# Key projection first, clears on ScalarE, feature blocks turned by TensorE and a contiguous routing stage in a hybrid S5 / RWKV-7 / MoE layer

## The chip, the core and the metric

The kernel runs on one core of a Trainium2 chip. The metric is the time of one execution in device microseconds, 1267.28 us before the change (median of 3 runs, 1266.63 to 1267.98). Below, PE is TensorE's matmul queue, PEld its weight loads, DVE is VectorE, ACT ScalarE, POOL GpSimd and SP SyncE, whose queue issues nearly all transfers.

## The reference

One decoder layer over 256 tokens of 1024 features, in f32:

```python
h = rms_norm(x, norm_mix_g)
proj = h @ w_in                       # columns: S5 input u, then r, k, v (512 each)
y_s5 = s5_mixer(proj[..., :r0], ...)  # 32 groups of 16 channels, 64 complex states each
y_rw = rwkv7_mixer(h, r, k, v, ...)   # 8 heads of 64: decay, iclr and gate LoRAs, delta rule
x = x + concat(y_s5, y_rw) @ w_out
x = x + moe_ffn(rms_norm(x, norm_moe_g), ...)   # top 4 of 32 experts, clamped SwiGLU
x = x + (p @ ple_w_proj) * sigmoid(rms_norm(x, norm_ple_g) @ ple_w_gate)
return rms_norm(x, final_norm_g)
```

The mixture computes every expert's three 1024x1024 f32 products for the tokens routed to it, so all 32 experts' weights are read (12 MB each).

## The kernel before, in words

The program is written by hand: each engine has its own list of instructions in the order of the code, and semaphores tie them. `layer` is the part up to the router's first logits; `experts` holds the routing stage, the loop over the experts and the tail, as three blocks, each of which begins when all engines have left the one before. All data lie in one on-chip array, `arena`, of 47 units of 1024 floats per partition; `un(i, n)` is n units from i, and names share units one after the other.

Head: SP loads the parameters, x transposed, the constants, then the eight quarters of `w_in` in the table `order` with the LoRA weights behind the second. POOL clears the padded S5 operands (L307 to L309) and, after the second projection, the taps (L317). ACT squares x (L325), computes step sizes and phases; DVE works out the S5 coefficients in many 16-element instructions (from L496) and inverts the root (L550). PE sums the squares with the ones of the constants.

Projections: `project(n)` makes quarter `order[n]`, `copy_proj(n)` on ACT moves it out of its bank. Before, the order is u, u, k, k, r, r, v, v. Between them PE does the LoRA products (all through banks 5 and 6), `kernel_taps` (the S5 output kernel, behind `o_padded`), `turn_g` (transposes the padded kernels, with an ACT copy of each), `stack_u` and `into` (S5 states' input). DVE runs `products` (S5 operands), `token_shift` (r, k, v with their predecessors), the decay's running sum, the normalised keys, `phase_off` and `phase_on` (rotation and scan of the S5 states, in two halves).

Scores: for 16 units (4 chunks of 64 tokens, 4 pairs of heads) PE computes five 64x64 products with `pair` (one product per head of the pair), DVE masks them. Then come five levels that invert a triangular matrix: per level and half PE makes W = MO X and Y W, ACT copies W, DVE adds to X and transposes it. Behind the levels 1 to 3, `turn` on DVE transposes bh, kh and v into `Bs`, `Ks`, `Vs` (L700, eight instructions each), and `s5_out` / `s5_y` make the S5 output. Then follow the scan over the four chunks, the normalisation of its output, `w_out` and the residual add (L795).

Routing (`experts`, first block): x normalised is split into three bf16 parts, written in the order that the weights' rows have ("run order"), so that the gather by one-hot matmuls is exact; `by_run` and `plain` are the two views. Tile 0 is split on DVE (`part`, L1210 to L1215), tile 1 by ACT (L1182 to L1190) and POOL (L1261, L1263). The logits are used at L1222 on DVE, then come the top 4, the mask (L1236), the ranks by a triangular matmul, and the number of passes (L1254). PE also makes three of the four products of the per-layer embedding (`ple_proj`), which ACT copies (L1193), and opens the output banks with products of zeros. SP loads the last two of the six weight chunks of expert 0.

Expert loop: each chunk of the ring is asked for again as soon as its matmuls are done:

```python
sp.wait_ge(s["chunks_used"], (n - 1) * NC + c + 1)
sp.dma_start(slot(c), chunk_src(c, e)).then_inc(chunk_in[c], 16)
```

## Time and profile before

| | |
|---|---|
| median of 3 runs | 1267.28 us |
| the profiled execution | 1267.05 us |
| its span | 1265.3 us |
| PE / PEld / DVE / ACT / POOL busy | 1170.8 / 514.8 / 402.3 / 205.1 / 28.3 us |
| routing block, from PE's first transpose | 260.76 us |
| PE's first loop matmul | 295.69 us |
| first load issued by the loop | 299.58 us |

Times in the rows are microseconds from the span's start. A row of the timeline gives start, duration, engine, line, operation, output and inputs with shapes, how often (x), and in brackets the idle time of the engine before it and who ended it. Durations of POOL are rough, and busy PE is not PE at its peak.

### The profile page before, as it was taken

The numbers are of one execution on the slowest core, as the hardware profiler recorded it, in microseconds if no ns is written. First come the engines' busy times: TensorE is split into PE (matmuls) and PEld (weight loads), VectorE is DVE, ScalarE is ACT, GpSimd is POOL, SyncE is SP. The second block draws the span as 40 slices with busy tenths as digits, with TensorE's granted clock in tenths as the row PEclk, the third lists the DMA queues.
The fourth block names the chain that finished last, engine by engine and source line by source line (L and its number), as shares of the span: only waits on it lengthen the run. The fifth ranks groups of instructions, "written<-read, shape, count | busy, mean of one in ns | idle before, by whom it ended". The sixth has DMA issues, their size and how long they took to land. (4 is left out here: it accounts for less than half of the span.)

```text
span 1265.3 us, 19269 instructions
## 1 busy us (share of the span) xinstructions
PE 1170.8 (93%) x8190; PEld 514.8 (41%) x8190; DVE 402.3 (32%) x750; ACT 205.1 (16%) x297; POOL 28.3 (2%) x16
## 2 busy tenths in 40 slices
PE   5889688958999999999999999999999999999997
PEld 4678586433333333333333333333333333333333
DVE  8928992572112122122112112211212112211222
ACT  2661012262000010011000001000011000000113
POOL 4100000020000000000000000000000000000000
PEclk8899888979999999999999999999999999999998
DMA  9300207235999999999999999999999999999960
GB/s 326 99 2 3 71 19 292 100 146 223 419 427 426 429 429 428 428 429 428 427 429 430 427 428 430 428 428 429 429 427 429 429 428 427 430 428 427 429 273 33
DMA packets 44237, 429.38 MB, mean 339 GB/s; under 512 B 4817, under 2 KB 15441, under 8 KB 19633
## 3 DMA queue, kind: packets, MB, share of 16 engines
q1 hardware_dynamic: 44016, 428.43, 80.9%
q8 instruction: 23, 0.38, 0.1%
q0 software_dynamic: 192, 0.52, 0.1%
q14 instruction: 6, 0.04, 0.0%
HBM read 427.89 MB, written 1.05 MB: 339 GB/s over the span
## 5 line engine op out<-in xcount | busy, mean ns | idle before, releaser
L1140 PE MATMUL bank<-arena 128*64 128x512 f32 (+5 forms) x5388 | 920.6, 479 | 24.7 <-DMA arena<-in_exp_w_up 19.1
L1140 PEld LDWEIGHTS bank<-arena 128*64 128x64 f32 (+4 forms) x5388 | 316.3, 128 | 605.3 <-issue 541.9
L221 PE MATMUL bank<-arena 64*64 64x64 f32 (+7 forms) x2032 | 175.0, 282 | 27.2 <-DVE arena L603 7.8
L221 PEld LDWEIGHTS bank<-arena 64*64 64x64 f32 (+3 forms) x2032 | 141.6, 160 | 59.8 <-issue 40.8
L1331 ACT ACTIVATE arena<-arena 128x512 f32<-128x512 f32 x32 | 20.1, 629 | 515.4 <-DVE arena L1375 515.4
L1390 DVE COPY arena<-bank 128x512 f32<-128x512 f32 x32 | 22.1, 691 | 234.9 <-PE bank L1140 234.9
L1380 DVE TENSOR_SCALAR arena<-bank 128x512 f32<-128x512 f32 x32 | 22.1, 691 | 211.8 <-PE bank L1140 211.8
L1375 DVE TENSOR_SCALAR arena<-bank 128x512 f32<-128x512 f32 x32 | 22.1, 691 | 188.8 <-PE bank L1140 188.8
L1334 ACT ACTIVATE arena<-bank 128x256 f32<-128x256 f32 x32 | 12.3, 383 | 310.1 <-PE bank L1430 310.1
L1351 DVE TENSOR_TENSOR arena<-bank,par 128x512 f32<-128x512 f32 x33 | 22.8, 692 | 76.4 <-PE bank L1140 76.4
L1331 ACT ACT_TABLE_LOAD x32 | 41.1, 1283 | 1.7 <-PEq L1162 1.2
L1383 DVE SCALAR_TENSOR_TENSOR arena<-arena 128x512 f32<-128x512 f32 x32 | 33.7, 1054 | 1.1
L1378 DVE TENSOR_TENSOR arena<-arena 128x512 f32<-128x512 f32 x32 | 22.1, 692 | 24.5 <-ACT arena L1331 24.5
L221 PE MATMUL bank<-arena,con 128*32 128x64 f32 (+2 forms) x160 | 17.5, 302 | 12.6 <-DMA con<-in_consts 10.4
L1336 ACT ACTIVATE arena<-bank 128x512 f32<-128x512 f32 x32 | 19.1, 597 | 1.7
L1363 DVE TENSOR_SCALAR arena<-con,arena 128x128 f32<-128x128 f32 x64 | 19.3, 344 | 0.0
L1434 PE MATMUL bank<-con,arena 128*128 128x128 f32 x128 | 19.2, 273 | 0.0
L1348 DVE TENSOR_SCALAR arena<-con,arena 128x64 bf16<-128x64 f32 x66 | 13.8, 251 | 13.3 <-DVE arena L1369 7.0
L700 DVE STREAM_TRANSPOSE arena<-arena 32x512 f32<-32x512 f32 x24 | 16.7, 697 | 0.3
L1430 PEld LDWEIGHTS bank<-con,arena 128*128 128x128 f32 x64 | 6.4, 141 | 24.3 <-issue 24.3
L221 PEld LDWEIGHTS bank<-arena,con 128*32 128x32 f32 (+1 forms) x160 | 9.5, 138 | 16.6 <-DMA con<-in_consts 10.4
L439 ACT ACTIVATE arena<-bank 128x512 f32<-128x512 f32 x10 | 6.0, 597 | 57.5 <-PE bank L221 57.5
(269 smaller groups left out, 459.8 us busy)
## 6 DMA issues: line engine op xcount, KB each, us to landing
arena<-in_exp_w_gate SPq DMA_DIRECT2D x64, 2048.0 KB, 23.4
arena<-in_exp_w_down SPq DMA_DIRECT2D x64, 2048.0 KB, 21.8
arena<-in_exp_w_up SPq DMA_DIRECT2D x64, 2048.0 KB, 25.3
arena<-in_w_in SPq DMA_DIRECT2D x8, 1024.0 KB, 12.1
arena<-in_w_out SPq DMA_DIRECT2D x4, 1024.0 KB, 5.5
arena<-in_ple_w_gate SPq DMA_DIRECT2D x2, 2048.0 KB, 21.7
arena<-in_xT SPq DMA_DIRECT2D x1, 1024.0 KB, 6.1
arena<-in_lora SPq DMA_DIRECT2D x1, 1024.0 KB, 13.6
```

Of the source, the lines that this page charges most:

```text
L221: return nc.tensor.matmul(out, lhsT, rhs, start=start, stop=stop, skip_group_check=True)
L1140: return nc.tensor.matmul(out, lhsT, rhs, start=start, stop=stop, skip_group_check=True)
L1331: nc.scalar.activation(sg, gt, ACT.Sigmoid, scale=1.702).then_inc(s["sig_ready"], 1)
L1336: nc.scalar.activation(actT[:, :, :, :], GATE[:, :].rearrange("p (k h s) -> p k h s", h=2, k=4), ACT.Copy).then_inc(s["actT_ready"], 1)
L1351: tt(xg[:, :, :], GAT[:, :].rearrange("p (k s) -> p k s", k=KD), prm("g_moe_run")[:, :, None].to_broadcast([P, KD, SLOTS]), ALU.mult).then ...
L1363: ts(pg[:, t, :], iota, rank[:, t, bass.ds(e, 1)], gates[:, t, bass.ds(e, 1)], ALU.is_equal, ALU.mult).then_inc(s["pg_ready"], 1)
L1375: ts(gt, GATE[:, :], 7.0, None, ALU.min).then_inc(s["gt_ready"], 1)
L1378: tt(sg, sg, gt, ALU.mult).then_inc(s["swish_ready"], 1)
L1380: ts(up, UP[:, :], 7.0, -7.0, ALU.min, ALU.max).then_inc(s["up_read"], 1)
L1383: stt(by_run(gt), plain(up), 1.0, plain(sg), ALU.add, ALU.mult).then_inc(s["act_ready"], 1)
L1390: V.tensor_copy(y, YB[:, :]).then_inc(s["y_ready"], 1)
L1434: last = nc.tensor.transpose(GATE[:, k * P:(k + 1) * P], gt[:, k * P:(k + 1) * P], ident)
```

## The change

It touches `layer` and the first block of `experts`, in nine pieces.

1. The order of the quarters becomes k, k, u, u, r, r, v, v. All waits that name a place in it go by `at_place`.
2. All clears leave POOL. ACT writes zeros (`clear`): a copy of the epsilon column times 0. Two are ahead of the step sizes, one between the exponentials, two behind the squares, the taps' one behind the output padding. The squares now stand behind the phases.
3. PE sums squares with ones that DVE writes (`ones_early`), not those of the constants.
4. The LoRA's second products use banks 5/6, 2/3, 5/6; the third stands behind `project(2)`. The key norms' sums stand behind `project(3)`; taps, turns, stack and both `into` stand behind `project(5)`.
5. ACT and DVE follow: on ACT the square of the keys, the decay's exponentials and the key norms' root come ahead of the output padding and the phases' sines; on DVE keys, decay and k2 come ahead of the output `products` (whose units change to 37, 25, 39), and `phase_off(0)`, `phase_on(0)` come behind r.
6. `turn` moves to PE (behind Y W of the levels 0, 1, 2), with ACT copying out of banks 0 and 1.
7. ACT adds the root of each tile's mean square to the square (`x2_root`); DVE splits tile 0 between its residual adds: one float write in run order, then contiguous casts and subtracts.
8. In the routing block DVE does the same for tile 1 (two casts on ACT), POOL does nothing there.
9. `ple_proj(0)` comes ahead of the logits, `ple_proj(1)` and `(2)` ahead of the ranks, each in a bank of its own; the products of zeros come last.

```diff
-        order = [0, 1, 4, 5, 2, 3, 6, 7]
+        LORA_BANK = (5, 2, 5)
+        order = [4, 5, 0, 1, 2, 3, 6, 7]
+        at_place = [order.index(q) + 1 for q in range(8)]
...
-                nc.gpsimd.memset(un(45), 0.0).then_inc(s["pads_clear"], 1)
-                nc.gpsimd.memset(un(16, 4), 0.0).then_inc(s["pads_clear"], 1)
-                nc.gpsimd.memset(un(20, 4), 0.0).then_inc(s["pads_clear"], 1)
...
+                def clear(a, n):
+                    A(un(a, n), par[:, NPARAM:NPARAM + 1].to_broadcast([P, n * UNIT]), ACT.Copy, scale=0.0).then_inc(s["pads_clear"], 1)
+                act.wait_ge(s["eps_ready"], 1)
+                clear(45, 1)
+                clear(16, 2)
...
+                clear(18, 2)
...
+                act.wait_ge(s["xT_in"], 16)
+                for b in range(2):
+                    A(sq[:, 4 * b:4 * b + 4, :], xT[:, 4 * b:4 * b + 4, :], ACT.Square).then_inc(s["sq_ready"], 1)
+                clear(20, 2)
+                clear(22, 2)
...
+                    if lev < 3:
+                        for b in range(2):
+                            act.wait_ge(s["turn_done"], 2 * lev + b + 1)
+                            A((Bs, Ks, Vs)[lev][:, 8 * b:8 * b + 8, :], banks[b].rearrange("p (u t) -> p u t", t=CH), ACT.Copy).then_inc(s["turned"], 1)
...
-                    A(un(33 + t), x2[:, t, :], ACT.Square, accum_out=ssq[:, t:t + 1])
+                    link(A(xn[t], x2[:, t, :], ACT.Square, accum_out=ssq[:, t:t + 1]))
+                    A(inv[:, t:t + 1], ssq[:, t:t + 1], ACT.Sqrt, bias=par[:, NPARAM:NPARAM + 1], scale=1.0 / D).then_inc(s["x2_root"], 1)
...
+                residual(0)
+                residual(1)
+                dve.wait_ge(s["x2_root"], 1)
+                link(V.reciprocal(inv[:, 0:1], inv[:, 0:1]))
+                link(ts(by_run(xn[0]), plain(x2[:, 0, :]), inv[:, 0:1], None, ALU.mult))
+                residual(2)
+                link(V.tensor_copy(parts[:, 0, 0, :], xn[0]))
+                link(tt(xres[0], xn[0], parts[:, 0, 0, :], ALU.subtract))
+                link(V.tensor_copy(parts[:, 0, 1, :], xres[0]))
+                tt(xres[0], xres[0], parts[:, 0, 1, :], ALU.subtract)
+                residual(3)
...
+                lora_second(0)
+                lora_second(1)
                 project(2)
+                lora_second(2)
+                project(3)
+                head_sums(kksq, 4).then_inc(s["kk_summed"], 1)
+                project(4)
+                project(5)
                 kernel_taps()
                 turn_g()
                 stack_u()
-                project(3)
                 into(0)
                 into(1)
...
+                def turn(n):
+                    if n == 0:
+                        pe.wait_ge(s["bonus_ready"], 1)
+                    pe.wait_ge(s["scaled"], 4)
+                    for b in range(2):
+                        if n:
+                            pe.wait_ge(s["turned"], 2 * n - 2 + b + 1)
+                        for u in range(8 * b, 8 * b + 8):
+                            last = pair(banks[b][:, (u % 8) * CH:(u % 8 + 1) * CH], fm((bh, kh, vv)[n], u), con[:, C_ID2:C_ID2 + CH])
+                        last.then_inc(s["turn_done"], 1)
...
+            nc.scalar.activation(parts[:, 0, 2, :], xres[0], ACT.Copy)
             act.wait_ge(s["rest_ready"], 1)
-            nc.scalar.activation(by_run(parts[:, 1, 1, :]), plain(xres[:, 1, :]), ACT.Copy).then_inc(s["parted"], 1)
+            nc.scalar.activation(parts[:, 1, 1, :], xres[1], ACT.Copy).then_inc(s["parted"], 1)
```

PE's list around the second LoRA products and the projections that follow. `win_in_*` are the quarters' loads. Before:

```order
L221 MATMUL bank<-lora_hidden,arena 128x256 [waits lora_hidden_ready]
L221 MATMUL bank<-lora_hidden,arena 128x256 x3
L221 MATMUL bank<-lora_hidden,arena 128x256 [waits lora2_copied,lora_hidden_ready]
L221 MATMUL bank<-lora_hidden,arena 128x256
L221 MATMUL bank<-lora_hidden,arena 128x256 [waits lora2_copied]
```

and with the change:

```order
L231 MATMUL bank<-lora_hidden,arena 128x256 [waits lora_hidden_ready]
L231 MATMUL bank<-lora_hidden,arena 128x256 x3
L231 MATMUL bank<-lora_hidden,arena 128x256 [waits lora_hidden_ready]
L231 MATMUL bank<-lora_hidden,arena 128x256 x3
L231 MATMUL bank<-arena 128x256 [waits proj_copied,win_in_u0]
L231 MATMUL bank<-arena 128x256 x15
L231 MATMUL bank<-lora_hidden,arena 128x256 [waits lora2_copied,lora_hidden_ready]
L231 MATMUL bank<-lora_hidden,arena 128x256
```

The second kind no longer waits for `lora2_copied`, and u's first quarter stands ahead of the third.

DVE's list in level 1 (L688 and L709 the masks, L745 and L756 the additions to X, L624 and L637 `s5_y`). Before:

```order
L688 TENSOR_TENSOR arena<-arena,con 128x512 [waits w_done] x2
L745 TENSOR_TENSOR arena<-arena,bank 128x512 [waits xy_done]
L692 STREAM_TRANSPOSE arena<-arena 128x512 [waits xy_ready]
L745 TENSOR_TENSOR arena<-arena,bank 128x512 [waits xy_done]
L692 STREAM_TRANSPOSE arena<-arena 128x512 [waits xy_ready]
L700 STREAM_TRANSPOSE arena<-arena 32x4x4x32 x8
L624 SCALAR_TENSOR_TENSOR arena<-arena,par,bank 128x4x64 [waits s5_out_done]
```

and with the change:

```order
L709 TENSOR_TENSOR arena<-arena,con 128x512 [waits w_done] x2
L756 TENSOR_TENSOR arena<-arena,bank 128x512 [waits xy_done]
L713 STREAM_TRANSPOSE arena<-arena 128x512 [waits xy_ready]
L756 TENSOR_TENSOR arena<-arena,bank 128x512 [waits xy_done]
L713 STREAM_TRANSPOSE arena<-arena 128x512 [waits xy_ready]
L637 SCALAR_TENSOR_TENSOR arena<-arena,par,bank 128x4x64 [waits s5_out_done]
```

The eight transposes of L700 are gone; PE's list has 32 products of 64x64 with `con` as moving operand in their place.

DVE's list from the last residual adds to the logits. Before:

```order
L795 TENSOR_TENSOR arena<-arena,bank 128x512 [waits out_done,x_in]
L795 TENSOR_TENSOR arena<-arena,bank 128x512 [waits out_done] x3
...
L1210 TENSOR_SCALAR arena<-arena 128x1024
L1211 CAST arena<-arena 128x2x128x4 [waits m_dve]
L1212 TENSOR_TENSOR arena<-arena 128x1024 [waits m_dve]
L1213 CAST arena<-arena 128x2x128x4 [waits m_dve]
L1214 TENSOR_TENSOR arena<-arena 128x1024 [waits m_dve]
L1215 CAST arena<-arena 128x2x128x4 [waits m_dve]
L1222 SCALAR_TENSOR_TENSOR arena<-bank,arena 128x32 [waits m_logits_done,m_router_in,m_dve]
```

and with the change, in the routing block:

```order
L1235 RECIPROCAL small<-small 128x1
L1236 TENSOR_SCALAR arena<-arena,small 128x2x128x4 [waits m_dve]
L1237 CAST arena<-arena 128x1024 [waits m_dve]
L1238 TENSOR_TENSOR arena<-arena 128x1024 [waits m_dve]
L1243 SCALAR_TENSOR_TENSOR arena<-bank,small,arena 128x32 [waits m_logits_done,m_router_in]
```

Three casts in run order became one float write in run order and one contiguous cast; the rest stands ahead of the fourth residual add or behind the mask.

## Rows read from the trace of the kernel before

**Rows 1.** Windows by stage: stretch, length; busy us (x) of PE, PEld, DVE, ACT, POOL; clock; DMA share; GB/s
```profile
260.00:290.00 30.00, 14.71 (x52) 8.81 (x52) 24.07 (x35) 20.39 (x21) 7.68 (x2) 0.66 0.41 154
...
321.00:600.00 279.00, 279.00 (x1690) 99.31 (x1688) 57.57 (x130) 28.92 (x40) 0.00 (x0) 1.00 1.00 427
```

**Rows 2.** Timeline of the head: start, duration, engine, line, operation, out<-in [idle before]
```profile
2.74 8.70 DVE L496 TENSOR_SCALAR s5p<-par 128x16 f32<-128x16 f32 x1 [1.82 <-DMA par<-in_params]
...
7.88 3.53 POOL L309 MEMSET arena<- 128x4096 f32 x1
...
10.36 6.55 PE L221 MATMUL bank<-arena,con 128*128 128x256 f32 x16 [10.36 <-DMA con<-in_consts]
...
18.84 1.75 DVE L550 RECIPROCAL arena<-arena 128x256 f32<-128x256 f32 x1
```

**Rows 3.** Timeline of the projections and the first scores
```profile
55.72 3.75 PE L221 MATMUL bank<-lora_hidden,arena 128*128 128x256 f32 x8 [3.88 <-ACT arena L372]
...
89.48 1.22 DVE L630 TENSOR_TENSOR arena<-arena 128x1020 f32<-128x1020 f32 x1 [22.82 <-ACT arena L358]
...
105.93 0.69 DVE L663 TENSOR_SCALAR arena<-arena 128x1024 f32<-128x1024 f32 x1 [5.15 <-ACT arena L432]
...
119.18 2.33 DVE L613 TENSOR_TENSOR_SCAN arena<-arena 128x512 f32<-128x512 f32 x2
...
125.34 0.60 ACT L358 ACTIVATE arena<-bank 128x512 f32<-128x512 f32 x1 [6.31 <-PE bank L221]
...
134.91 0.68 DVE L713 TENSOR_TENSOR arena<-bank,con 128x512 f32<-128x512 f32 x1
...
135.14 9.41 PE L221 MATMUL bank<-arena 64*64 64x64 f32 x256 [7.82 <-DVE arena L603]
```

**Rows 4.** Timeline of the levels, and the start of the chunk scan
```profile
158.93 11.75 PE L221 MATMUL bank<-arena 64*64 64x64 f32 x328 [2.00 <-DVE arena L745]
...
166.24 5.68 DVE L700 STREAM_TRANSPOSE arena<-arena 32x512 f32<-32x512 f32 x8
...
176.31 5.67 DVE L700 STREAM_TRANSPOSE arena<-arena 32x512 f32<-32x512 f32 x8
...
195.89 1.97 PE L221 MATMUL bank<-arena 64*64 64x64 f32 x32 [5.29 <-ACT arena L441]
```

**Rows 5.** Windows of PE: stretch, length, busy us (x records), granted clock, DMA share, GB/s
```profile
56.00:58.00 2.00, 2.00 (x6) 0.50 0.00 0
...
161.00:162.00 1.00, 1.00 (x24) 0.50 0.00 0
...
169.00:170.00 1.00, 1.00 (x41) 1.00 0.00 0
```

**Rows 6.** Timeline of the routing stage and the loop's start
```profile
258.60 0.69 DVE L795 TENSOR_TENSOR arena<-arena,bank 128x512 f32<-128x512 f32 x1 [3.62 <-PE bank L221]
...
268.32 2.74 DVE L1213 CAST arena<-arena 128x1024 bf16<-128x1024 f32 x1
...
278.15 0.41 DVE L1222 SCALAR_TENSOR_TENSOR arena<-bank,arena 128x32 f32<-128x32 f32 x2
...
278.92 2.40 DVE L1227 TENSOR_SCALAR arena<-arena 128x2 f32<-128x2 f32 x1
...
286.19 0.15 DVE L1254 TENSOR_SCALAR arena<-arena 128x1 int32<-128x1 f32 x1
...
278.44 2.85 POOL L1263 TENSOR_TENSOR arena<-arena 128x1024 f32<-128x1024 f32 x1 [4.89 <-ACT arena L1184]
...
285.15 5.67 PE L1140 MATMUL bank<-arena,lora_hidden 128*128 128x512 f32 x8
...
290.86 0.60 ACT L1193 ACTIVATE arena<-bank 128x512 f32<-128x512 f32 x1 [1.32 <-PE bank L1140]
...
295.69 18.03 PE L1140 MATMUL bank<-arena 128*64 128x512 f32 x80 [0.87 <-DVE arena L1351]
```

**Rows 7.** The page's costliest groups: one run-order write in the loop
```profile
L1383 DVE SCALAR_TENSOR_TENSOR arena<-arena 128x512 f32<-128x512 f32 x32 | 33.7, 1054 | 1.1
```

More of the change, by code:

```diff
@@ L679, in _ @@
                 V.memset(state[:, :], 0.0)
+                phase_off(0)
+                phase_on(0)
                 phase_off(1)
@@ L908, in _, with head_sums @@
                             last.then_inc(s["lora2_done"], 1)
-                project(2)
+                def head_sums(src, bank):
+                    for b in range(2):
+                        last = mm(banks[bank + b][:, :], head_ones, src[:, 2 * b:2 * b + 2, :], True, True)
+                    return last
+                lora_second(0)
+                lora_second(1)
+                project(2)
+                lora_second(2)
+                project(3)
+                pe.wait_ge(s["consts_in"], 16)
+                pe.wait_ge(s["kk_squared"], 1)
+                pe.wait_ge(s["lora2_copied"], 6)
+                head_sums(kksq, 4).then_inc(s["kk_summed"], 1)
+                project(4)
+                project(5)
                 kernel_taps()
@@ L1277, in _ @@
             last.then_inc(s["logits_done"], 1)
-            pe.wait_ge(p_in, 32)
-            ple_proj(0, banks[5]).then_inc(s["ple_done"], 1)
+            for n in range(1, EARLY):
+                ple_proj(n, banks[n]).then_inc(s["ple_done"], 1)
             pe.wait_ge(s["mask_ready"], 1)
```

233 lines of the change are left out of this document (98 added, 135 removed).

## The prediction

> **What bounds the kernel now.** I read the page's 40 slices first: from slice 11 on, DMA stands at 9 and TensorE at 9, before that neither does. The table of stages says it in numbers [rows 1]: in the expert loop PE is busy 279.00 of 279.00 us at a granted clock of 1.00, and the DMA engines' share is 1.00. The change leaves every line of that loop and of the tail as it is, and the loop's loads are released by its own matmuls, so the loop moves as a block: **what counts is when it begins**, 295.69 us before [rows 6]. Then I read the timeline of each engine from 0 to 296 us and asked at each hand-over which engine came last. There are four places.
>
> First, the head. VectorE's second useful instruction, 16 elements wide, takes 8.70 us, and ends where POOL's last clear ends (7.88 + 3.53 = 11.41) [rows 2]. VectorE's chain of small instructions follows, and the first reciprocal starts at 18.84, though ScalarE's root was there earlier.
> Second, the projections. VectorE idles 22.82 us for the keys' copy, until 89.48; PE idles 3.88 us before 55.72, behind ScalarE, and then runs at a clock of 0.50 [rows 3, 5]. PE ends the projections at 125.3, and after the first scores waits 7.82 us until 135.14 for VectorE, whose score masks start at 134.91 [rows 3].
> Third, the inversion's levels. PE waits at each for VectorE, 2.00 us at the second, and VectorE has eight 32-row transposes there, 5.68 us a time, three times [rows 4]. After each wait PE runs at 0.50 (1.2 of 2.4 GHz): 24 records a microsecond against 41 at 1.00 [rows 5].
> Fourth, routing. The logits' first use on VectorE is at 278.15, behind casts of 2.74 us into run order; then ScalarE's last copy at 290.86 waits for PE's late small projections (8 records, 5.67 us) [rows 6]. The mean clock there is 0.66 [rows 1].
>
> **The head.** ScalarE now clears 1024 + 2048 + 2048 elements before its squares and 4096 behind them. At 0.60 us for 512 (the last copy [rows 6]) that is about 1 us per 1024. It clears from 2.0 to 5.0, then one exponential, 2.0 more of clearing, two exponentials, a table load of 1.3 and two sines: the squares run 9.5 to 11.5 instead of from 7.4. PE no longer waits for the constants; it starts at the first half, 10.6 instead of 10.36, takes the same 6.55 [rows 2], and the root is out at 17.7. VectorE, without the 8.70 us, is done by 14.5. So the reciprocal starts at 17.7 instead of 18.84: **-1.1 us**. This queue is a new wait: ScalarE's clears are in front of the squares. Bounds 0 (if the 8.70 us stays) and -2.
>
> **The projections.** PE's queue keeps the work and loses the holes: the second LoRA products of the first two kinds go to banks of their own, the third stands behind a projection. Gone are 3.88 us of idling, some 2.9 us lost at 0.50 behind it [rows 5], and 1.1 us of small gaps. What stays is the hole while ScalarE empties the transposed kernels. With the head, PE ends the projections 9.0 us earlier: 116.3.
> Is anything else later? I laid the changed lists of all engines against each other, with the durations that the same instructions have in the timeline. ScalarE: exponentials of the decay to 65, the root of the key norms at 69.3, padding of the S5 outputs to 73.6, clear to 75.5, sines and copies to 83.1; PE reaches the taps at 81.3, so o_padded is 7 us early and the last copy (83.1) is in time for its reader, VectorE's r. VectorE: g products to 46.7, then keys 51, decay 56.3, k2 59.5, output products 67, phase angles 72.8, then the chain that took 105.93 to 119.18 [rows 3], 13.25 us: 86.0. r and its products to 91.9. Then it waits: PE's first into() ends at 99.3. phase_off(0), phase_on(0), phase_off(1) take 3.8 + 6.4 + 3.7: 113.2, before PE's 116.3. So PE sets the masks' start, 1.0 us of first scores later: 117.4 instead of 134.91, **-17.5 us** with the head. PE feeds the masks at the pace of before, and the levels start at 131.6. Bound above: if VectorE is late after all, only PE's wait of 7.82 us comes back; below: -19.
>
> **The levels.** VectorE loses 3 x 5.68 us. PE gains 3 x 64 records (32 products of 64x64, two records each), at 41 a microsecond 1.56 us each, and ScalarE six copies of 0.6 us. Per level at full clock: 64 + 64 records, 64 more for the turn, and s5_out at 2.45 us, together 7.1 us instead of the 10.1 at which VectorE repeats (eight transposes at 166.24, the next at 176.31 [rows 4]). VectorE's own part is 4.7 (two masks, two additions, two transposes, s5_y), so PE has no hole once it is in step. From 131.6: level 0 at half clock to 136.3, turn and s5_out to 140.3, a wait of 1.2 us for X, which phase_on(1) holds back as before; level 1 to 149.3, level 2 to 156.4, level 3 to 162.0, level 4 to 165.1, VectorE to 166.5, Gelu to 167.6. The chunk scan starts at 168.0; I add 0.9 us, half of what another fall of the clock in level 1 costs, 168.9 instead of 195.89 [rows 4]: **another -9.5 us**. Bounds: all levels at half clock, 2.7 us a turn and 11.5 us a level, give nothing; no fall at all -10.5. I take the upper end of speed, since PE runs on through each level.
> The Trainium skill weighs against this (VectorE: DVE Perf Modes, "The three transpose paths" and "Rules for kernel authors"): a bf16 block of 128x128 takes 390 ns on TensorE and 311 ns on VectorE, and 32x32 blocks within a bank are fastest on VectorE. By that ratio 5.68 us would become 7.1 us of PE per turn. The rows of PE's small products (41 a microsecond) say 1.56, and the sum goes by them. The mechanism is a rival below.
>
> Chunk scan, normalisation and output projection are unchanged, so -27.0 holds to there. The weights they need are asked for earlier, and DMA is nearly idle.
>
> **Routing.** Times here on the clock of before. The last residual add was at 258.60 [rows 6]. Now VectorE has, between the second and the fourth: waiting for ScalarE's square and root of tile 0 until 253.1, a reciprocal, one run-order write, the third add, two contiguous casts and two subtracts. The write's nearest row is the loop's own run-order write, 1054 ns for 512 elements [rows 7], so 2.05 us for 1024; ends 0.69 (a plain one-input instruction of that size, first row of the 13.25 us chain [rows 3]) and 2.74 (the cast [rows 6]). A contiguous cast: 0.7 by that plain row, at most 2.74. Subtracts 1.23. The fourth add starts at 260.1: **+1.5**, and ScalarE's root behind its square adds 0.4: the block starts 1.9 later, 262.65. The third add is 1.1 late and nobody waits for it.
> In the block VectorE clears 0.9, writes 2.05, casts 0.7, subtracts 1.23: free at 267.7. PE: transposes, the first small projection now ahead of the logits, partly at 0.50 after its hole of 2.4 us (3.5 us full at that clock, 1.7 at 1.00), logits done at about 268.6. So the logits are used at 268.7 instead of 278.15. From there the mask took 4.8 us, of which 2.2 were one 2-element instruction of 2.40 us beside POOL's subtract, which is gone [rows 6]: 271.2. One more subtract 1.23, then 1.9, the ranks, 0.9: count at 275.2. PE in the meantime: two projections at 1.00 to 272.0, ranks to 273.6, the four clears of banks to 274.6 (they wait for ScalarE's third copy, 272.7). ScalarE's casts are 1.1 each instead of 4.8. The block ends at 275.2 instead of 291.46, and the hand-over to the loop, 4.2 us (290.86 + 0.60 to 295.69), stays: **-16.3 us**. Bounds: run-order writes at 2.74 and all at 0.50: -11; writes at 0.69: -19.
> A second rule of the skill (the same page, "Mode 2x_2P"): a one-input instruction between SBUF tensors runs two elements a cycle whatever the stride if the outer dimension is even. By it both writes would take 0.69 and the sum would be 2.7 us lower, 1221. The old casts with the same pattern took 2.74 [rows 6], so the trace does not agree.
>
> **Sum.** -17.5 - 9.5 - 16.3 = -43.3 us. The profiled execution took 1267.05 (span 1265.3 and 1.75 around it), 0.2 under the median of the three runs, 1267.28. 1267.1 - 43.3 = 1223.8, rounded to **1224**.
>
> **The rivals.**
> *VectorE still comes last before the scores* (phase_off(0) and everything behind it is now queued behind r, and into(0) behind two more projections). For: a margin of only 3 us in a chain of 70. Against: the rows' durations add up. It gives back up to the 7.82 us wait and a clock fall: 1233. Chance 0.10.
> *Casts stay slow* although contiguous, because it was the bf16 write and not the stride. Against: I find no contiguous f32 to bf16 cast in this trace, but float writes in run order are slow too [rows 7]. Two casts of 2.7 in front of the fourth add, one in the block, three of 4.8 on ScalarE in line with VectorE's: +10 us, 1234. Chance 0.09.
> *Turns are as dear on PE as on VectorE*: if 16 blocks of small products, their bank switches and the wait for ScalarE's copy take 5.68 us on PE too, a level is 5.6 + 5.68 = 11.2 us instead of 7.1, +12.3 over three: 1236. Against: 41 records a microsecond [rows 5]. Chance 0.03. By the ratio in the skill's table it would be 7.1 us a turn and 1241.
> *The change does not reach the end*: the loop's end would have to be fixed by its loads and not by its start. But the first load of the loop waits for the first chunk's matmuls, so it moves too; within 0.2%, chance 0.01.
> *Slower*: the loop itself loses the full clock. It runs PE without a gap [rows 1], so each microsecond at 0.50 costs nearly half a microsecond; 43 us are gone if the clock is at 0.50 for 87 us or more of the loop, and slower begins beyond about 92. At 120 us of it the kernel takes 1284. For it: PE now is busier in the 160 us ahead of the loop. Against: 1.00 throughout 321 to 600 us, and every fall of the clock in this trace follows a hole in PE's work. Chance 0.02.
>
> **How the numbers follow.** The forecast has 0.75, with its own ends 1217 (writes at 0.69, no clock fall) and 1230 (slow writes, half of the levels' gain). The range reaches to the first two rivals: 1217 to 1236. Faster by over 0.2% (2.5 us, about what can be told from no change): 0.97; within: 0.01; slower: 0.02.
>
> **What would show it.** VectorE's second instruction under 0.3 us and the reciprocal near 17.7; no hole of PE between 50 and 81; masks of the scores near 117.4, with PE, not VectorE, the last; a granted clock of 1.00 from level 1 on and 64 turn records in about 1.6 us; chunk scan near 169; logits used about 6 us after the block's start, against 17.4 before; contiguous casts near 0.7; PE's loop from 252.4 on. Wrong it would be if a wait on `into_done` or `phase_off` stands ahead of the scores, if casts keep 2.7 us, or if PE's wait of 2 us per level stays.

## The result, and the profile after

The changed kernel takes **1222.65 us** (median of 4 runs, 1220.94 to 1226.11), the kernel before, run beside it, 1267.63 (4 runs, 1266.63 to 1268.09): ratio 0.965, 95% interval 0.9625 to 0.9675. Forecast were 1224.0, range 1217 to 1236. The profiled execution took 1220.94 us (span 1219.2), 46.1 under the profiled one before, against -43.3 in the sum. So the total came out 2.9 us below the sum for that execution; its parts were off by more, in both directions.

The head, timeline of the changed kernel (start, duration, engine, line, operation, out<-in, count, [idle before <- who ended it]):

```profile
2.69 0.17 DVE L518 TENSOR_SCALAR s5p<-par 128x16 f32<-128x16 f32 x1 [1.66 <-DMA par<-in_params]
...
16.49 1.75 DVE L572 RECIPROCAL arena<-arena 128x256 f32<-128x256 f32 x1 [2.31 <-ACT arena L350]
...
2.04 2.85 ACT L330 ACTIVATE arena<-par 128x1024 f32<-128x1024 f32 x2
...
8.98 1.99 ACT L346 ACTIVATE arena<-arena 128x1024 f32<-128x1024 f32 x2
...
10.16 5.71 PE L231 MATMUL bank<-arena 128*128 128x256 f32 x16 [10.16 <-ACT arena L346]
```

The 8.70 us instruction of [rows 2] is down to 0.17. The reciprocal starts at 16.49 instead of 18.84, and now waits for ScalarE's root, as forecast (17.7). ScalarE's queue of clears is the new wait; it came 0.5 us earlier than the 9.5 I gave it.

Projections and first scores, timeline after:

```profile
97.90 0.69 DVE L611 TENSOR_TENSOR arena<-bank,arena 128x512 f32<-128x512 f32 x1 [2.27 <-PE bank L231]
...
108.53 0.69 DVE L611 TENSOR_TENSOR arena<-bank,arena 128x512 f32<-128x512 f32 x1 [0.27 <-PE bank L231]
...
115.34 0.60 ACT L372 ACTIVATE arena<-bank 128x512 f32<-128x512 f32 x1 [6.31 <-PE bank L231]
...
116.43 0.69 DVE L724 TENSOR_TENSOR arena<-bank,con 128x512 f32<-128x512 f32 x1 [4.08 <-PE bank L231]
```

The last copy of a projection is at 115.34 instead of 125.34, the first score mask at 116.43 instead of 134.91 [rows 3]. The bracket decides the first rival: VectorE waits 4.08 us for PE there, so VectorE is not last.

The levels, PE's timeline after:

```profile
130.24 5.50 PE L231 MATMUL bank<-arena 64*64 64x64 f32 x128 [3.54 <-DVE arena L709]
135.54 2.06 PE L231 MATMUL bank<-con,arena 64*64 64x64 f32 x64
...
141.42 3.02 PE L231 MATMUL bank<-arena 64*64 64x64 f32 x96 [0.17 <-DVE arena L756]
144.27 2.03 PE L231 MATMUL bank<-con,arena 64*64 64x64 f32 x64
...
152.38 2.03 PE L231 MATMUL bank<-con,arena 64*64 64x64 f32 x64
...
169.55 1.15 PE L231 MATMUL bank<-arena 64*64 64x64 f32 x32 [2.66 <-ACT arena L461]
```

The rows of inputs `con,arena` are the turns. The second and the third lie 8.11 us apart: that is the period of a level now, against 10.07 between the transposes of [rows 4]. The chunk scan starts at 169.55 instead of 195.89.

Windows of the two kernels. First before (busy us (x) of PE, PEld, DVE, ACT, POOL; granted clock; DMA share; GB/s):

```profile
20.00:48.00 28.00, 26.74 (x114) 21.13 (x115) 27.76 (x34) 5.72 (x7) 10.28 (x3) 0.89 0.80 257
...
195.00:200.00 5.00, 4.11 (x51) 3.84 (x52) 0.00 (x0) 0.93 (x2) 0.00 (x0) 0.50 1.02 433
...
235.00:240.00 5.00, 5.00 (x10) 2.18 (x9) 4.86 (x8) 0.69 (x1) 0.00 (x0) 0.70 1.07 453
```

and after, the same places of the program where they now lie, and the loop's entry:

```profile
20.00:48.00 28.00, 25.88 (x125) 20.46 (x123) 27.50 (x33) 6.27 (x11) 8.18 (x2) 1.00 0.80 258
...
168.00:173.00 5.00, 3.45 (x56) 2.94 (x56) 0.21 (x1) 1.44 (x2) 0.00 (x0) 1.00 1.02 412
...
205.00:210.00 5.00, 4.15 (x10) 2.00 (x11) 4.74 (x6) 1.48 (x3) 0.00 (x0) 1.00 1.04 437
...
246.00:250.00 4.00, 3.13 (x26) 1.25 (x24) 1.87 (x8) 0.00 (x0) 0.00 (x0) 0.55 0.34 114
250.00:254.00 4.00, 4.00 (x14) 1.26 (x12) 0.00 (x0) 0.00 (x0) 0.00 (x0) 0.60 0.00 0
```

The clock's column tells of two things that were not in the forecast. PE runs at 1.00 through the chunk scan and the start of the output projection, where it had 0.50 and 0.70. And it is at 0.55 to 0.60 at the loop's entry, behind a wait of 3.29 us, which costs there.

Routing and loop start, timeline after:

```profile
223.17 1.28 DVE L809 TENSOR_SCALAR arena<-arena,small 128x1024 f32<-128x1024 f32 x1
...
225.09 0.69 DVE L811 CAST arena<-arena 128x1024 bf16<-128x1024 f32 x1
...
236.42 0.41 DVE L1243 SCALAR_TENSOR_TENSOR arena<-bank,small,arena 128x32 f32<-128x32 f32 x2 [0.68 <-PE bank L1172]
...
237.19 0.17 DVE L1248 TENSOR_SCALAR arena<-arena 128x2 f32<-128x2 f32 x1
...
242.68 0.15 DVE L1277 TENSOR_SCALAR arena<-arena 128x1 int32<-128x1 f32 x1
...
245.01 1.62 PE L1172 MATMUL bank<-arena 128*128 128x64 bf16 x48 [3.29 <-DVE arena L1363]
...
247.49 20.85 PE L1172 MATMUL bank<-arena 128*64 128x512 f32 x80 [0.87 <-DVE arena L1366]
```

A contiguous cast takes 0.69 us against 2.74 [rows 6], the float write in run order 1.28, the 2-element instruction 0.17 against 2.40. The loop's products start at 247.49 instead of 295.69, but their first group takes 20.85 us instead of 18.03 [rows 6].

### The profile page after: what moved, and what is told of

Read it like the earlier page. It is cut to its first block and busy times, and to the rows that moved or that the text cites. A ratio compares the mean times of both kernels' runs of the same rounds, so it can differ in the third digit from the quotient of the medians.

```text
span 1219.2 us, 19644 instructions
## 1 busy us (share of the span) xinstructions
PE 1157.3 (95%) x8382; PEld 506.1 (42%) x8382; DVE 368.9 (30%) x730; ACT 207.3 (17%) x310; POOL 10.7 (1%) x10
## 5 line engine op out<-in xcount | busy, mean ns | idle before, releaser
L231 PE MATMUL bank<-arena 64*64 64x64 f32 (+7 forms) x2048 | 169.1, 267 | 22.6 <-ACT arena L346 10.2
L231 PEld LDWEIGHTS bank<-arena 64*64 64x64 f32 (+3 forms) x2048 | 135.5, 147 | 53.9 <-issue 40.1
L1351 ACT ACTIVATE arena<-bank 128x512 f32<-128x512 f32 x32 | 19.1, 598 | 1.7
L1449 PE MATMUL bank<-con,arena 128*128 128x128 f32 x128 | 19.2, 273 | 0.0
L1445 PEld LDWEIGHTS bank<-con,arena 128*128 128x128 f32 x64 | 6.4, 141 | 24.3 <-issue 24.3
L1449 PEld LDWEIGHTS bank<-con,arena 128*128 128x128 f32 x128 | 15.0, 140 | 0.0
L582 DVE SCALAR_TENSOR_TENSOR arena<-arena,par 128x256 f32<-128x256 f32 x16 | 14.1, 952 | 0.0
L1445 PE MATMUL bank<-con,arena 128*128 128x128 f32 x64 | 14.0, 301 | 0.0
L231 PE MATMUL bank<-arena,con 128*32 128x64 f32 (+1 forms) x144 | 10.3, 264 | 2.2 <-ACT arena L484 1.4
```

The costliest lines, as they stand in the source:

```text
L231: return nc.tensor.matmul(out, lhsT, rhs, start=start, stop=stop, skip_group_check=True)
L1445: last = nc.tensor.transpose(YB[:, t * P:(t + 1) * P], pg[:, t, :], ident)
L1449: last = nc.tensor.transpose(GATE[:, k * P:(k + 1) * P], gt[:, k * P:(k + 1) * P], ident)
```

## The experiments

The marks of all profiled executions, in us from each span's start. "Masks" is VectorE's first score mask, "scan" PE's first product of the chunk scan, "turn x2" PE's first transpose of the residual stream, "loop" the start of the loop's first group of float products, "group" how long that group of 80 records took. The ratios are to the runs of the kernel before that were taken beside each kernel (medians 1266.1 to 1267.6), and of each edit only the telling lines are printed. One profile is one execution: in `x2`, `x8` and `x12`, whose code up to the scores' products is that of the changed kernel, the masks start 0.7 to 0.9 us later than in it, with PE at 0.94 over 20 to 48 us (`x2`, `x12`) or 0.83 over 84 to 94 (`x8`), so a mark that moves by less than 1 us says nothing.

| kernel | masks | scan | turn x2 | loop | group | median (runs) | ratio to before, 95% |
|---|---|---|---|---|---|---|---|
| before | 134.91 | 195.89 | 254.09 | 295.69 | 18.03 | 1267.63 (4) | |
| after | 116.43 | 169.55 | 223.97 | 247.49 | 20.85 | 1222.65 (4) | 0.965 [0.9625, 0.9675] |
| xb, before + projections | 118.91 | 179.41 | 237.55 | 279.17 | 18.03 | 1249.94 (4) | 0.9861 [0.9845, 0.9878] |
| x5, before + turns on PE | 134.36 | 187.85 | 242.28 | 285.60 | 18.03 | 1256.63 (4) | 0.9918 [0.9901, 0.9934] |
| x4, before + routing | 134.78 | 195.80 | 254.01 | 279.59 | 18.03 | 1250.48 (4) | 0.9875 [0.9858, 0.9891] |
| x1, after - head | 119.47 | 172.97 | 228.94 | 253.51 | 20.42 | 1226.12 (4) | 0.9671 [0.9655, 0.9687] |
| x2, after - turns | 117.29 | 178.02 | 235.05 | 259.29 | 18.03 | 1230.88 (4) | 0.9715 [0.9699, 0.9731] |
| x3, after - routing | 116.48 | 169.60 | 224.02 | 267.28 | 18.03 | 1239.10 (4) | 0.9781 [0.9765, 0.9797] |
| x11, after, old PE order in routing | 116.39 | 169.52 | 223.94 | 254.99 | 20.58 | 1229.06 (4) | 0.970 [0.9685, 0.9716] |
| x9, before + scan kept busy | 135.01 | 195.84 | 250.27 | 292.08 | 18.03 | 1264.11 (10) | 0.998 [0.997, 0.999] |
| x6, after + hole filled | 113.44 | 167.13 | 224.77 | 250.68 | 20.73 | 1220.08 (4) | 0.9626 [0.961, 0.9642] |
| x8, after + turns earlier | 117.18 | 168.44 | 224.56 | 250.50 | 20.84 | 1224.41 (4) | 0.9662 [0.9647, 0.9677] |
| x12, after + kept busy | 117.30 | 171.33 | 227.45 | 254.51 | 18.03 | 1224.92 (5) | 0.9672 [0.9659, 0.9685] |
| x13, x6 + x8 + x12 | 113.45 | 165.61 | 220.03 | 245.78 | 18.03 | 1218.97 (5) | 0.963 [0.9617, 0.9644] |

**One part at a time on the kernel before.** `xb` takes only pieces 1, 4 and 5 of the change:

```diff
-        order = [0, 1, 4, 5, 2, 3, 6, 7]
+        LORA_BANK = (5, 2, 5)
+        order = [4, 5, 0, 1, 2, 3, 6, 7]
```

> The kernel before with only the projections' part of the change: keys first, the new order of PE, VectorE and ScalarE up to the scores; old head, old turns, old routing. Theory (of the 18.5 us that the scores start earlier, 2.4 belong to the head): the score masks start at about 118.8 instead of 134.9 us, total 16 to 17 us under before, 1250.5 to 1251.5, and up to 2 us less than that if the old levels wait longer. Rival (VectorE's eight transposes and the clock take part of it back): the gain at the masks is there, but under 10 us of it at the end.

Masks at 118.91, ratio 0.9861 (-17.6 us). The theory holds, with a total 0.6 us under the foretold range: 16.0 of the 18.5 us at the masks are the projections'. The levels cost what they did before: from masks to scan 60.5 us against 61.0.

`x5` takes only piece 6, in DVE's levels:

```diff
-                    if lev in (1, 2, 3):
-                        turn(*((Bs, bh), (Ks, kh), (Vs, vv))[lev - 1])
```

> The kernel before with only the turns of bh, kh and v moved to PE. Theory: each level is 2.0 us shorter and one turn of 5.7 us less for VectorE behind 2.0 us of PE's; chunk scan 7 to 8.5 us earlier, total 1258.5 to 1260. Rival (PE, not VectorE, was the slower one in the levels, and its added 192 records cost as much as they save): within 2 us of before.

More than expected: ratio 0.9918, -10.4 us. The scan starts 8.0 us earlier, as foretold. The rest came behind it: scan to the turning of x2 takes 54.4 us instead of 58.2, though nothing there was edited. The scan's products behind the first 32 of [rows 4], timeline of PE before, then in `x5` with the first 32:

```profile
197.62 1.09 PE L221 MATMUL bank<-rec,arena 64*64 64x64 f32 x16
198.65 2.86 PE L221 MATMUL bank<-arena 128*128 128x256 f32 x8
```

```profile
187.85 1.15 PE L221 MATMUL bank<-arena 64*64 64x64 f32 x32 [2.65 <-ACT arena L445]
188.81 0.66 PE L221 MATMUL bank<-rec,arena 64*64 64x64 f32 x16
189.40 1.99 PE L221 MATMUL bank<-arena 128*128 128x256 f32 x8
```

With the shorter wait in front (2.65 us instead of 5.29) the same 32 products take 1.15 us and not 1.97. Whether the clock is the cause of the 3.8 us, or only falls with it, `x9` tries below.

`x4` takes only pieces 7 to 9, the routing part:

```diff
-            nc.scalar.activation(by_run(parts[:, 1, 0, :]), plain(xn[:, 1, :]), ACT.Copy).then_inc(s["parted"], 1)
+            link(ts(by_run(xn[1]), plain(x2[:, 1, :]), inv[:, 1:2], None, ALU.mult))
+            link(V.tensor_copy(parts[:, 1, 0, :], xn[1]))
```

> The kernel before with only the routing part of the change. Theory (the routing gain does not depend on the rest): from residual to the loop's first matmul 18 us less, total 1248.5 to 1251; the parts then add up: this, the projections alone (1249.9) and the turns alone sum to the whole within 3 us. Rival (the gain needs the earlier start of the weights and of PE): under 14 us.

Ratio 0.9875, -15.8 us; the loop starts 16.1 us earlier, all of it behind the turning of x2. That is 2 us less than the theory's 18 at the loop's start, though the total lies in the foretold range: here PE was at half clock behind its hole at the block's start (first small projection 3.03 us, in the changed kernel 1.88), and at half clock again in the gather ahead of the loop (2.72 us, in the changed kernel 1.62). The parts add up: 17.6 + 10.4 + 15.8 and 2.7 for the head (0.9671 against 0.965) are 46.5 us, the whole is 44.4, with 2 to 3 us of uncertainty on each.

**One part at a time off the changed kernel.** `x1` undoes the head:

```diff
+                nc.gpsimd.memset(un(45), 0.0).then_inc(s["pads_clear"], 1)
+                nc.gpsimd.memset(un(16, 4), 0.0).then_inc(s["pads_clear"], 1)
+                nc.gpsimd.memset(un(20, 4), 0.0).then_inc(s["pads_clear"], 1)
```

> The changed kernel with only the head put back: the clears of the padded tiles on POOL again, ScalarE's two squares first in its queue. Theory (the clears on POOL hold VectorE's second instruction, and the reciprocal behind it): that TENSOR_SCALAR takes about 8.7 us again instead of 0.17, the reciprocal starts near 18.8 us instead of 16.5, and everything behind it is 1.0 to 2.4 us later, total 1223.7 to 1225.1. Rival (the head is slack, since PE catches up with its loads later): the projections end where they do now, 0 us, 1222.6.

Its timeline shows the instruction and POOL's last clear ending together again, at 11.44 and 11.41:

```profile
2.68 8.76 DVE L518 TENSOR_SCALAR s5p<-par 128x16 f32<-128x16 f32 x1 [1.65 <-DMA par<-in_params]
...
18.84 1.75 DVE L572 RECIPROCAL arena<-arena 128x256 f32<-128x256 f32 x1
...
7.88 3.53 POOL L321 MEMSET arena<- 128x4096 f32 x1
```

The reciprocal is at 18.84 to the hundredth, the masks 3.0 us later, the median 3.5 (by the ratios 2.7), 1.0 above the foretold range. More than the 2.35 us of the reciprocal: without the head's change PE's clock over 20 to 48 us is 0.89, as before, and with it 1.00 (0.94 in `x2` and `x12`). In this profile the clock also fell behind the wait at the scan, which is as long as in the changed kernel (2.66 us): the first 32 products took 1.95 us. The rival, that the head is slack, is out.

`x2` gives the turns back to VectorE:

```diff
+                    if lev in (1, 2, 3):
+                        turn(*((Bs, bh), (Ks, kh), (Vs, vv))[lev - 1])
```

> The changed kernel with bh, kh and v turned by VectorE again. Theory (VectorE is the last at each level, and its turn of 5.7 us is on the path; PE's turn is 2.0 us in a time in which it mostly waited): the levels' period goes from 8.1 back to about 10.1 us, the chunk scan starts 7 to 9 us later (about 177.5 instead of 169.6), total 1229.6 to 1231.6. Rival (the gain of the levels came with the earlier projections and the clock, not with the turn): under 3 us.

+8.2 us, scan 8.5 later. PE's wait ahead of the scan is 6.83 us, and behind it the scan's first 32 products take 1.97 us, as in [rows 4].

`x3` puts the old routing back, the reverse of `x4`'s diff:

> The changed kernel with the routing stage and the residual additions of before. Theory (run-order bf16 casts of 2.74 and 4.8 us, the late small projections and the 2.40 us instruction come back): from the residual to the loop's first matmul 18 us more, first matmul near 265.5, less what a longer routing stage does for the clock at the loop's entry (its first group of 80 records then takes 18.0 instead of 20.85 us): total 1237.8 to 1240.7. Rival (the routing part was covered by other waits and the gain was the earlier start): under 12 us.

+16.5 us at the median, as written. The loop starts 19.8 us later (1.8 more than expected) and its first group takes 18.03 again, 2.8 less. The clock's fall is not gone there but earlier: the 48 gather products in front of the group take 2.72 us instead of 1.62.

`x11` keeps the contiguous casts and puts PE's small projections back where they stood:

```diff
-            ple_proj(0, banks[0]).then_inc(s["ple_done"], 1)
             pe.wait_ge(s["h_ready"], 1)
...
+            ple_proj(0, banks[0]).then_inc(s["ple_done"], 1)
+            for n in range(1, EARLY):
+                ple_proj(n, banks[n]).then_inc(s["ple_done"], 1)
```

> The changed kernel with PE's small projections in routing in the order of before (the first behind the logits, the other two behind the ranks); the casts stay contiguous. It tells how the 16 to 18 us of the routing part divide. Theory (most is the casts on VectorE and ScalarE and the 2-element instruction that no longer waits for POOL; the order of PE is worth what PE's queue then has behind the ranks): +2 to +4 us, 1224.7 to 1226.7. Rival (the late projections were the path, as the chain of before ends in ScalarE's last copy of them): +6 us or more.

Here my theory lost: +6.4 us, the rival's number. Its PE timeline:

```profile
231.37 1.06 PE L248 MATMUL bank<-con,arena 128*128 128x128 f32 x8 [1.25 <-PEq L268]
234.26 3.62 PE L1172 MATMUL bank<-arena 128*128 128x32 f32 x16 [1.83 <-ACT arena L1208]
237.70 3.76 PE L1172 MATMUL bank<-arena,lora_hidden 128*128 128x512 f32 x4
241.25 2.18 PE L1172 MATMUL bank<-arena,con 128*128 128x32 f32 x10
243.24 5.29 PE L1172 MATMUL bank<-arena,lora_hidden 128*128 128x512 f32 x8
```

With nothing to do in its 1.83 us wait for x2's copies, PE comes out of it at 0.50 and stays there until 246: the 16 products of the logits take 3.62 us instead of 1.97, the first small projection 3.76 instead of 1.88. And the other two stand behind the ranks. So of the 16.5 us of the routing part some 6 are PE's order (part work moved off the end, part clock), some 10 the casts and what ran beside POOL. That is more than the one instruction of [rows 6], as VectorE's and POOL's timelines of the kernel before show:

```profile
266.30 1.98 DVE L1212 TENSOR_TENSOR arena<-arena 128x1024 f32<-128x1024 f32 x1
...
271.09 4.25 DVE L1214 TENSOR_TENSOR arena<-arena 128x1024 f32<-128x1024 f32 x1
...
268.72 4.83 POOL L1261 TENSOR_TENSOR arena<-arena 128x1024 f32<-128x1024 f32 x1 [229.02 <-ACT arena L1182]
```

The subtract of L1214 has the form of that of L1212, and took 2.3 us longer; POOL's own subtract ended at 273.55, in the middle of it. In the changed kernel such a subtract takes 1.23 us, on contiguous operands and with POOL idle.

**Is it the clock?** `x9` adds products that nobody reads to the kernel before, in its wait ahead of the scan:

```diff
+                pe.wait_ge(s["w_copied"], 2 * LEVELS)
+                for _ in range(4):
+                    mm(banks[4][:, :], ident, con[:, 0:512], True, True)
                 pe.wait_ge(s["xy_ready"], 2 * LEVELS)
```

> The kernel before with four extra 128x512 float products of PE, written into a bank that nobody reads, in its wait of 5.3 us ahead of the chunk scan (the output is unchanged). Theory (the 3.8 us that the chunk scan to residual stretch lost without any edit there are the clock, 0.50 behind that wait in before and 1.00 in the changed kernel): the granted clock is 1.00 at the chunk scan's start and the stretch is 1.7 to 3.5 us shorter, total 1263.5 to 1265.5. Rival (it is the transfers of the weights, or the chain through VectorE): 0 to +0.5 us.

PE's timeline, with the added products first:

```profile
190.54 3.70 PE L221 MATMUL bank<-con 128*128 128x512 f32 x8
195.84 1.15 PE L221 MATMUL bank<-arena 64*64 64x64 f32 x32 [1.60 <-ACT arena L441]
```

and the windows of the same kernel, to be held against the two of before above:

```profile
195.00:200.00 5.00, 4.16 (x78) 3.64 (x80) 0.00 (x0) 0.97 (x2) 0.00 (x0) 1.00 0.99 423
...
235.00:240.00 5.00, 5.00 (x13) 2.13 (x13) 4.89 (x8) 0.00 (x0) 0.00 (x0) 1.00 0.63 265
```

The scan starts at the same time, its window reads 1.00 instead of 0.50, and the turning of x2 comes 3.8 us earlier, the same 54.4 us behind the scan as in the changed kernel. The transfers at the scan were as before (a share of 0.99 and 1.02), so that rival is out. Over ten runs the ratio is 0.998 [0.997, 0.999], -2.5 us: more work on PE, and faster. This is shown: the unforecast gain behind the levels is the clock.

The gain has two parts, though, and the wait at the scan explains the first alone. From the scan to PE's wait of 1.45 us ahead of the output projection it takes 36.3 us instead of 38.4, and from there to the turning of x2 18.1 instead of 19.8. In all four profiles with 5.14 to 6.83 us of idle ahead of the scan (before, `xb`, `x4`, `x2`) its first 32 products took 1.97 or 1.98 us; with 2.65 or 2.66 us they took 1.15 in five (after, `x3`, `x5`, `x8`, `x11`), but 1.95 in `x1` and 1.77 in `x6`. The wait ahead of the output projection is 1.45 us in all fourteen profiles, and the clock fell behind it in six (before, `xb`, `x4`, `x6`, `x8`, `x12`) and not in the other eight. So a shorter wait makes the fall rarer; it doesn't rule it out.

**What binds now?** `x6` moves seven products of the seventh projection into the hole where PE waits for ScalarE:

```diff
+                        if n == 1:
+                            project_part(6, 0, 5)
...
                 stack_u()
+                project_part(6, 5, 7)
                 into(0)
                 into(1)
-                project(6)
+                project_part(6, 7, 16)
```

> The changed kernel with seven of the projection products of group 6 moved into the hole in which PE waits for ScalarE's copies of the transposed kernels (84 to 94 us, PE busy 6.55 of 10 us). Theory (PE's queue sets the scores' start): the score masks start 2 to 2.8 us earlier, total 1219.8 to 1220.8. Rival (VectorE's chain up to phase_off(1), which ends at 112.3 against PE's 115.3, or ScalarE's copies are next at once): 0 to -1 us.

Masks at 113.44, 3.0 us earlier: PE's queue is the bound of the projections, as the forecast had it, and VectorE has 1.25 us left of its 4.08. The median fell by 2.6 to 1220.08, as foretold, in a range of 1218.13 to 1224.25 that overlaps that of the changed kernel. The profiled execution was the slowest: its clock fell behind the waits at the scan (0.74 over 165 to 170) and behind the routing block's, and gave the 3 us back.

`x8` turns bh ahead of level 0, in PE's wait for the masks:

```diff
+                turn(0)
                 for lev in range(LEVELS):
...
-                    if lev < 3:
-                        turn(lev)
+                    if lev < 2:
+                        turn(lev + 1)
```

> The changed kernel with the turn of bh on PE ahead of level 0, in the 3.5 us in which PE waits for VectorE's masks, that of kh at level 0 and that of v at level 1. Theory (PE's queue sets the period of the levels, 8.1 us, of which the turn is 2.0): level 0 starts at full clock (5.5 to about 3 us for its 128 records) and one turn leaves the chain, chunk scan 2 to 4.5 us earlier, total 1218 to 1220.7. Rival (VectorE's s5_y and phase_on or ScalarE's copies hold the levels): 0 to -1 us.

From masks to scan it takes 51.26 us instead of 53.12, about one turn of 2 us. Level 0 is faster, as the theory has it (its 128 records take 3.95 us instead of 5.50), but PE then waits 1.69 us for VectorE ahead of level 1, which is the rival's half of the story. The total shows no gain: 1224.41 (1221.95 to 1224.78) against 1220.94 to 1226.11, and above the 1218 to 1220.7 foretold. In the profile the clock fell behind the small waits at 204 us and 232 us (0.63 over 204 to 208, 0.57 over 232 to 236), where the changed kernel's profile has 1.00. Inconclusive in the total.

`x12` puts products that nobody reads in front of the scan and at the loop's entry:

```diff
+            for _ in range(4):
+                mm(banks[5][:, :], ident, con[:, 0:HF], True, True)
...
+            mm(banks[5][:, :], ident, con[:, 0:HF], True, True)
             pe.wait_ge(s["bias_in"], 48)
```

(and ahead of the scan the four of `x9`)

> The changed kernel with nine extra 128x512 float products of PE into banks that nobody reads, so that its output is the same: four in its wait ahead of the chunk scan (2.66 us), four behind the last product of the routing stage and one at the start of the loop's block (a wait of 3.29 us). Theory (PE's clock falls to 0.50 behind these waits and the run-to-run spread of 1221 to 1226 us is whether it falls at the scan as well): clock 1.00 at both places, the loop's first group of 80 records takes 18.0 instead of 20.85 us, scan to the turning of x2 54.4 us in every run, total 1218 to 1219.5 and a spread under 2.5 us. Rival (the clock at the loop's entry falls whatever PE does for a few us, or the added products push the gather back): 1222 to 1225, spread as before.

A miss that teaches. PE's timeline of `x12`:

```profile
167.70 3.70 PE L231 MATMUL bank<-con 128*128 128x512 f32 x8
171.33 1.15 PE L231 MATMUL bank<-arena 64*64 64x64 f32 x32
...
246.33 3.60 PE L1175 MATMUL bank<-con 128*128 128x512 f32 x8
251.12 1.12 PE L1175 MATMUL bank<-con 128*128 128x512 f32 x2 [1.19 <-PEq L1197]
252.08 1.56 PE L1175 MATMUL bank<-arena 128*128 128x64 bf16 x48
254.51 18.03 PE L1175 MATMUL bank<-arena 128*64 128x512 f32 x80 [0.87 <-DVE arena L1371]
```

The clock did what the theory says: the first group takes 18.03. But one such product takes 0.93 us (two records), so four are 3.70 us in waits of 2.66 and 3.29. No idle stands in front of the scan any more: it could have started at 167.70 + 2.66 = 170.36, and starts 1.0 later. The gather starts 5.6 us behind the routing block's last own product instead of 3.29, 2.3 later. 3.3 paid, 2.8 got; and the clock then fell behind the next wait, 1.45 us at 206 (56.1 us from scan to turning). And 2 us lie where nothing was edited: in this profile the clock had fallen over 20 to 48 us (0.94), and it fell behind the 1.28 us ahead of the routing block's first product (0.64 over 234 to 238). 1224.92 is the rival's number, and the interval lies above that of `x6`; it overlaps that of the changed kernel, so that the filler costs in the total is not clear of the noise.

`x13` is `x6`, `x8` and `x12` at once:

> The changed kernel with three edits at once: seven products of group 6 in PE's hole at 84 to 94 us, the turns one level earlier, and the nine extra products that keep PE busy ahead of the chunk scan and at the loop's entry. Theory (each lies in front of a different wait, so they add): -3.0, -2 to -4.5 and -3.5 to -4.5 us, total 1212 to 1215.5, and a spread under 2.5 us. Rival (they share the same slack, VectorE becomes last in projections and levels): no better than the best of them alone, 1218 or more.

1218.97 us (1217.09 to 1221.14), ratio 0.963: 3.7 us under the changed kernel's median, and so below both kernels, though the intervals still overlap. But it lies in the rival's figures, 1218 or more: by the ratios (0.963 against 0.9626, intervals overlapping) it is no better than `x6` alone. It misses the theory's 1212 to 1215.5 by about the 3.3 us that the added products of `x12` cost. In the profiled execution, the fastest of the five (1217.09), the clock is 0.997 and every stage has full speed. The same with one product fewer in each place wasn't tried.

## Why the prediction was right, step by step

The place was right: loop and tail move as a block. The loop's first group ends at 268.34 instead of 313.72, 45.4 us earlier, and the whole is 46.1 shorter. The terms, by the marks of the table:

| term | forecast | measured | what it was |
|---|---|---|---|
| head and projections, masks | -17.5 | -18.5 | projections 16.0, head 2.5 |
| levels, masks to scan | -9.5 | -7.9 | rate of small products misread |
| scan to turning of x2 | 0 | -3.8 | clock, not seen |
| routing, to the loop's start | -16.3 | -18.1 | run-order write mis-sized |
| the loop's first group | 0 | +2.8 | clock, not seen |

- **Head** (-1.1, measured -2.35 at the reciprocal): cause right, size half. The squares came 0.5 us earlier than my queue of ScalarE, and PE's sum took 5.71 us and not 6.55, the duration of [rows 2]. Not in the sum: PE's clock behind it, 1.00 over 20 to 48 us against 0.89.
- **Projections**: PE is busy without a hole from 48 to 84 us, and set the masks (bracket of 116.43, and `x6`). The rival with VectorE last is out, with 4.08 us to spare; I had given it 3.
- **Levels**: the mechanism held (the period fell, and the 2 us wait is gone), but "PE gains 3 x 64 records, at 41 a microsecond 1.56 us each" failed in its size. The 41 of [rows 5] are of products of the very same kind, counted wrongly: a window counts every record that touches it, also those that straddle its ends. The microseconds from 167 to 170 of that trace read 42, 41 and 41 one by one and 111 as a single window; less those that straddle its ends too, that is some 34 a microsecond. So it is in the changed kernel: the halves of a level, 32 records each, are handed over 0.94 us apart (149.79, 150.73, 151.66). The level from 144.27 on has 1.97 us for the turn (forecast 1.56), 2.36 for `s5_out` (2.45) and 3.78 for its 128 records (3.12): 8.11 instead of 7.1. Level 0 took 5.30 us where the sum has 4.7. The Trainium skill (VectorE: DVE Perf Modes, "The three transpose paths") has 390 ns on TensorE and 311 ns on VectorE for a bf16 block of 128x128, from which came the estimate of 7.1 us a turn; for these 64x64 float blocks the trace shows 2.03 against 5.68, so the ratio doesn't carry over, and its 1241 was out.
- **"Chunk scan, normalisation and output projection are unchanged, so -27.0 holds to there"**: this is the step that failed. Unchanged code ran 3.8 us faster because PE's clock was higher: 2.1 us of it behind a wait of 2.66 instead of 5.29 us (`x5`, `x9`), 1.7 behind a wait that had not changed (1.45 us), where what decided is open. [Rows 5] had shown me falls of the clock behind waits; I charged them inside the stages I edited and not in the one behind.
- **Routing**: contiguous casts 0.69, as taken. For the run-order write I took 2.05 us from a two-input instruction [rows 7]; a one-input one takes 1.28. The Trainium skill (the same page, "Mode 2x_2P") gives such an instruction two elements a cycle on conditions that name no stride, and I had read it as the contiguous speed, 0.69, whatever the stride; 1.28 lies between the two, and the measurement decides. The total came near the 1221 of that rule, but by other terms. The late logits of before I laid to the casts alone; 2.3 us of them was the subtract beside POOL (4.25 us against 1.98). That casts stay slow was the second rival: out.
- **The slower rival** named the clock in the loop; what came is its beginning only, 2.8 us, and from the 260th to the 290th microsecond the window reads 1.00.

The errors of the terms add to -1.0 + 1.6 - 3.8 - 1.8 + 2.8 = -2.2 us, and -0.7 in loop and tail. That the total came so close is partly luck: five errors of 1 to 4 us, in both directions, nearly cancel.

## What to carry to other kernels

A wait of PE costs its own length and often a slow stretch behind it, which may lie in code that nobody touched (2.1 us behind 5.29 us of waiting here); when a change shortens or makes such a wait, follow it into the next stage. Useful work put into a wait of PE (`ple_proj` ahead of the logits, a projection's products in `turn_g`'s hole) pays for both; filler (products that nobody reads) gained where it was shorter than the wait (3.70 in 5.29 us, `x9`) and pushed the work back where it was longer (3.70 in 2.66 and 3.29 us, `x12`), so read what one takes first. Take a rate from a long window or from starts, not from a window of a few record lengths, which counts the records at both its ends. And take the price of an operation from a row of the same kind, number of inputs and width, not from one that only shares its access pattern.

## What the runs showed of the hardware

- A float write in run order (out of order in memory, one input) of 128x1024 takes 1.28 us on VectorE, contiguous 0.69; the cast to bf16 in the same order took 2.74 [rows 6], contiguous 0.69. The order costs the 2-byte write 2.05 us and the 4-byte write 0.59.
- VectorE instructions that run beside POOL's can last until POOL is done. The 16-element one took 8.70 or 8.76 us while POOL cleared 9 units and 0.17 without; no other of its shape ran beside the clears. The 2-element one took 2.40 and ended at 281.32, POOL's subtract at 281.29. In the changed kernel it still happens: of the sixteen 128x256 instructions from 23.97 on (L582) two took 3.93 and 4.73 us, beside POOL's two instructions of 24.02 to 27.62 and 27.70 to 32.28, and the others some 0.4 to 0.5 us each; PE then waits 2.12 us for them. What it would gain to take these two from POOL was not tried.
- Holes decide PE's clock, but not alike in each execution. Behind the same 1.45 us wait ahead of the output projection it stayed at 1.00 in the changed kernel's profile and in seven others, and fell in six. At the loop's entry the first group took 20.42 to 20.85 us in the four profiles with a wait of 3.29 or 3.30 us ahead of the gather (after, `x1`, `x6`, `x8`) and 18.03 in those with 2.43 to 2.94, `x2` among them with the same code there; but in `x11`, with 2.43, 20.58. In `x2` to `x5` the gather itself took 2.72 us instead of 1.56 to 1.62, so there the fall came and went earlier. So the spread of 1221 to 1226 us fits the clock (mean 0.994 down to 0.989 in the four runs), but what decides in one execution stays open.
